# Differential attention on one core: the two softmaxes combined in chunks of 512 keys, spread over the steps of a round

## What is computed

```
sc = einsum('bqhd,bkhd->bhqk', qb, k) * scale         # 8 heads of 64, used in pairs
sc = where(k_chunk <= q_chunk, sc, lowest)            # causal by chunks of 64
pr = softmax(sc, axis=-1).reshape(b, 4, 2, 128, s)
a  = pr[:, :, 0] - lam * pr[:, :, 1]                  # two softmaxes, one difference
out = einsum('bhqk,bkhe->bqhe', a, v)                 # value width 128
```

## Time and profile before

| | |
|---|---|
| median of 3 runs | 1739.46 us (1738.71 to 1740.19) |
| the profiled execution | 1740.0 us, its span in the trace 1738.1 us |
| TensorE matmul busy | 1701.3 us, 98% of the span |
| TensorE weight loads busy | 1418.6 us, 82% |
| VectorE / ScalarE / GpSimd busy | 1087.6 / 665.6 / 272.3 us (63% / 38% / 16%) |
| granted TensorE clock | full speed (0.999) |
| attention, from its first score to its last gate product | about 779 to 1382 us |

### The profile page before, as it was taken

How to read it: one execution, slowest core, us unless ns; L and a number is a source line. 1 busy time by engine, 2 the same in 40 slices (tenths; PEclk the granted TensorE clock), 3 DMA queues, 4 the chain that set the end, 5 groups by cost and what they waited for, 6 DMA issues and landing times.

```text
span 1738.1 us, 22885 instructions
## 1 busy us (share of the span) xinstructions
PE 1701.3 (98%) x8296; PEld 1418.6 (82%) x8296; DVE 1087.6 (63%) x2151; ACT 665.6 (38%) x1184; POOL 272.3 (16%) x194
## 2 busy tenths in 40 slices
PE   7999999999999999999999998999999899999998
PEld 6888888888788888888888887888888788888887
DVE  5538566645877877747777776777867453424242
ACT  5423233224333323215455454554555442323231
POOL 0000000265522332311110022111111040000000
PEclk9999999999999999999999999999999999999999
DMA  7447999754425433297677558856567865353532
GB/s 242 139 162 298 384 350 335 251 155 144 146 76 167 120 99 114 80 293 242 197 202 233 137 165 247 248 172 179 167 176 224 290 232 189 109 182 112 180 111 71
DMA packets 161886, 331.04 MB, mean 190 GB/s; under 512 B 15714, under 2 KB 60770, under 8 KB 156258
## 3 DMA queue, kind: packets, MB, share of 16 engines
q1 hardware_dynamic: 160610, 327.38, 59.4%
q10 hardware_dynamic: 1152, 2.10, 0.3%
HBM read 218.26 MB, written 111.16 MB: 190 GB/s over the span
## 4 chain that ended last, share of the span: by engine, by line
PE 87%; DVE 5%; DMA 3%; issue 2%; POOL 1%; ACT 1%; SPq 1%; DVEq 0%; ACTq 0%
PE bank L1245 14%; PE bank L1246 14%; PE bank L1247 14%; PE bank L1422 13%; PE bank L1327 5%; PE bank L1329 5%; PE bank L1330 5%; PE bank L1382 5%; PE bank L1354 3%; PE bank L1355 3%; PE bank L1365 3%; DVE e L2181 2%; DVE at_lo L2217 1%; PE bank L1255 1%; PE bank L1402 1%
## 5 line engine op out<-in xcount | busy, mean ns | idle before, releaser
L1327 PE MATMUL bank<-ht,a_op 128*128 128x512 f32 x504 | 196.3, 390 | 2.4 <-DVE stage L1958 1.2
L1330 PE MATMUL bank<-ht,a_op 128*128 128x512 f32 x504 | 196.1, 389 | 0.0
L1329 PE MATMUL bank<-ht,a_op 128*128 128x512 f32 x504 | 196.1, 389 | 0.0
L1720 ACT ACTIVATE e<-e,nbias 128x128 f32<-128x128 f32 (+15 forms) x128 | 153.6, 1200 | 80.7 <-DVE nbias L2190 80.6
L2181 DVE CUSTOM_DVE_ANT_0 e<-bank,zeros 128x512 f32<-128x512 f32 x192 | 124.9, 688 | 90.3 <-PE bank L1355 90.1
L1245 PE MATMUL bank<-ht,w 128*128 128x512 f32 x448 | 174.4, 389 | 0.0
L1246 PE MATMUL bank<-ht,w 128*128 128x512 f32 x448 | 174.3, 389 | 0.0
L1247 PE MATMUL bank<-ht,w 128*128 128x512 f32 x448 | 174.3, 389 | 0.0
L1422 PE MATMUL bank<-ht,w 128*128 128x512 f32 x624 | 168.7, 395 | 0.0
L1229 POOL TENSOR_SCALAR mask<-kc,qc 128x128 f32<-128x128 f32 (+3 forms) x64 | 87.7, 1370 | 495.8 <-DVE mx L2181 495.3
L1382 PE MATMUL bank<-at_hi,v_sl 128*128 128x256 f32 (+1 forms) x576 | 118.9, 285 | 14.7 <-DVE at_lo L2217 14.2
(11 more groups left out here) (188 smaller groups left out, 3515.7 us busy)
## 6 DMA issues: line engine op xcount, KB each, us to landing
w<-split_s SPq DMA_DIRECT2D x92, 512.0 KB, 4.8
raw<-in_w_in SPq DMA_DIRECT2D x64, 512.0 KB, 5.4
split_s<-piece SPq DMA_DIRECT2D x24, 1024.0 KB, 5.7
q_st<-qk_s SPq DMA_DIRECT2D x128, 128.0 KB, 4.9
ring<-gate_s SPq DMA_DIRECT2D x64, 256.0 KB, 3.4
ht_s<-ht SPq DMA_DIRECT2D x6, 2048.0 KB, 9.5
gate_s<-gate_st SPq DMA_DIRECT2D x48, 256.0 KB, 4.9
qk_s<-stage SPq DMA_DIRECT2D x48, 192.0 KB, 3.9
```

The source lines that it names most:

```text
L1327: nc.tensor.matmul(out[:], hi, right[:, k, 0, :], start=k == 0 and not adds, stop=False, skip_group_check=adds)
L1329: nc.tensor.matmul(out[:], hi, right[:, k, 1, :], start=False, stop=False, skip_group_check=adds)
L1330: mm = nc.tensor.matmul(out[:], lo, right[:, k, 0, :], start=False, stop=k == 3, skip_group_check=adds)
L1720: nc.scalar.activation(e, e, ACT.Exp, bias=nbias[G % 2][:, h:h + 1], scale=SCALE, accum_out=esum[G % 2][:, h:h + 1]).then_inc(exp_done, 1)
```

## The change

The combine of tile R is cut into its chunks. Chunk 0 (with the reciprocal and the ratio) stays at step 1; chunk i goes to step i+1, behind that step's `at_split`, but to the last step where the round has no step i+1. A turn now waits for its own chunk's combine, and the counters are counted in chunks instead of tiles.

```diff
 def turn(G, c, wide):
-    if c == 0:
-        pe.wait_ge(combined, G + 1)
     o = plan.before(G) + c // BLK
+    pe.wait_ge(combined, o + 1)
...
 def mask_max(G, c, wide, h):
-        dve.wait_ge(combined, G - 1)
+        dve.wait_ge(combined, plan.before(G - 1))
...
-def combine(G):
-    s1, s2 = esum[G % 2][:, 0:1], esum[G % 2][:, 1:2]
-    dve.wait_ge(exp_done, 2 * (G + 1))
-    nc.vector.reciprocal(ratio[:, 0:1], s2).then_inc(recip_done, 1)
...
-    a, b = e1[G % 2][:, 0:plan.keys(G)], e2[G % 2][:, 0:plan.keys(G)]
+def combine(G, c, wide):
+    if c == 0:
+        s1, s2 = esum[G % 2][:, 0:1], esum[G % 2][:, 1:2]
+        dve.wait_ge(exp_done, 2 * (G + 1))
+        nc.vector.reciprocal(ratio[:, 0:1], s2).then_inc(recip_done, 1)
...
+    a, b = e1[G % 2][:, c:c + wide], e2[G % 2][:, c:c + wide]
     nc.vector.scalar_tensor_tensor(out=a, in0=b, scalar=ratio[:, 1:2], in1=a, op0=ALU.mult,
                                    op1=ALU.add).then_inc(combined, 1)
...
-                        if 0 <= R < TILES and j == min(1, len(steps) - 1):
-                            combine(R)
+                        for i, chunk in enumerate(plan.chunks(R) if 0 <= R < TILES else ()):
+                            if j == min(i + 1, len(steps) - 1):
+                                combine(R, *chunk)
```

More of the change, by code:

```diff
@@ L2190, in neg_max @@
                     nc.vector.tensor_scalar(nbias[G % 2][:], m2[:], -SCALE, None, ALU.mult).then_inc(nb_ready, 1)
-                def combine(G):
-                    s1, s2 = esum[G % 2][:, 0:1], esum[G % 2][:, 1:2]
-                    dve.wait_ge(exp_done, 2 * (G + 1))
-                    nc.vector.reciprocal(ratio[:, 0:1], s2).then_inc(recip_done, 1)
[L2196 to L2199, removed]
-                    a, b = e1[G % 2][:, 0:plan.keys(G)], e2[G % 2][:, 0:plan.keys(G)]
+                def combine(G, c, wide):
[3 more added lines that the diff above has]
+                        nc.vector.reciprocal(ratio[:, 0:1], s2).then_inc(recip_done, 1)
+                        dve.wait_ge(recip_done, G + 1)
+                        nc.vector.scalar_tensor_tensor(out=ratio[:, 1:2], in0=ratio[:, 0:1], scalar=lam[:, 0:1], in1=s1,
+                                                       op0=ALU.mult, op1=ALU.mult).then_inc(ratio_ready, 1)
+                        dve.wait_ge(ratio_ready, G + 1)
+                    a, b = e1[G % 2][:, c:c + wide], e2[G % 2][:, c:c + wide]
                     nc.vector.scalar_tensor_tensor(out=a, in0=b, scalar=ratio[:, 1:2], in1=a, op0=ALU.mult,
```

## The result

The changed kernel takes 1742.82 us in the median of 21 runs (1740.05 to 1747.4), the kernel before, on the same chip at the same time, 1740.19 us (21 runs, 1736.37 to 1745.25). The ratio is 1.0017, with a 95% interval of 1.0009 to 1.0024: **slightly slower, by 3 us on the mean**, where -0.3 us was forecast. The time lies in the forecast range; its sign is that of neither my own case nor its rival C. The profiled executions differ by much less than the runs do: 1740.56 us (span 1738.7) against 1740.0 (span 1738.1).

A forecast was written before the change was run, and what follows sets the result against it. TensorE was taken as the bound, with only 28 us of waits for `at_lo` to win. A gain of 10.5 us and a loss of 10.2 us gave -0.3 us, forecast 1739.2 us, range 1733 to 1745.

The forecast's parts named there:

- my own case: Whole kernel: gain and loss nearly cancel, -0.3 us, reaching from -5 to +4; chance 0.65, no sign claimed.
- rival C: Step 1 of even rounds: the bias's lateness is taken up, the 10.5 us gain remains, 1729 us; chance 0.17.
- What bounds the kernel: Attention: time can come only from TensorE's waits, 28.0 us in 38 waits of the values for `at_lo`.
- The price of a piece: Combine on VectorE: a cut costs 0.13 us (bounds 0 to 0.22); 96 more instructions, 12.5 us more VectorE.
- What goes away: Step 3 of even rounds: values' waits behind the whole combine go, 5.25 us per half, 10.5 us in all.
- What comes in: End of odd rounds: last pieces delay the bias and next even round's values, 5.3 and 4.9 us, 10.2 us loss.
- Even rounds' later bias: End of even rounds: bias 0.4 to 0.7 us later, covered in odd rounds; uncovered, up to 8 us.
- The sum: Whole kernel: -10.5 + 10.2 = -0.3 us, forecast 1739.2 us.
- kind two: Step 1 of even rounds: values of chunk 0 wait for a split chained from the round before; rest of the 28 us.
- A: Start of rounds 8 to 24: reserves not to be had, 9.0 us per half reach the values, +7.5, 1747 us; chance 0.15.
- B: End of odd rounds: GpSimd's mask blocks the pieces on VectorE, 14*1.6 = 22 us, 1761; chance 0.03.
- D: Attention: nothing happens, pieces still run one behind another, 1739 us; counted with my own case, 0.65.

The follow-up runs named there:

- bias first: Changed kernel, but in odd rounds the last step's pieces are combined after `neg_max`, `scaled_eps` and `norm_o`; 1741.5 us, 1.0009 to the kernel before.
- cut only: Combine cut into pieces as in the change, but all pieces together at step 1; 1748.14 us, ratio 1.0052 to the kernel before.
- the earlier load: Load of `z_in` issued one round earlier, at the top of the odd round: kernel before 1740.03 us (0.9997), changed kernel 1744.87 us (1.0024).

## Why the prediction was right or wrong, step by step

- **What bounds the kernel: right.** The attention's time is in the waits for `at_lo`, and the runs that move them move the time: 19.6 us of them at 1732.6 us, 27.5 at 1742.8, 32.8 at 1748.1, 37.3 at 1752.9. It is no law to a few us: the kernel before has 28.0 at 1740.2, bias first 23.9 at 1741.5. And "no other wait of the attention counts for much" was wrong, see the sum below.
- **The price of a piece: right.** 0.12 to 0.14 us for a cut in the run with the cuts alone (forecast 0.13); 14.0 us more busy time for 96 instructions (forecast 12.5). The Trainium skill (VectorE: DVE Perf Modes, section on the TRN2 errata) is right in direction, that many small tiles pay a latency each time. The 60 ns that I took from its table are half of what the trace shows for this instruction, and the section itself says that this row comes out too low.
- **What goes away: right, 9.8 us for 10.5.** Six of the eight waits a half are gone. In round 20 0.34 us stay (forecast 0.32), in round 24 0.22 of 0.22: I had counted that one as gone.
- **What comes in: right, 10.7 us for 10.2.** Rounds 14, 16 and 18 wait 1.51, 2.15 and 1.91 us (forecast 1.4, 2.0 and 1.7), counting the scores' part. The claim that a wait at the scores would mean I was wrong was too strict: it appeared (2.7 us in six waits), but it lies in front of the same values and is a part of the same lateness. What it does show is that VectorE itself is late, not only ScalarE, as the run with the bias first confirms.
- **Even rounds' later bias: harmless, as said.** It was to come 0.4 to 0.7 us later. In the kernel with even rounds alone it comes 1.1 to 1.4 us later behind the last mask_max of rounds 8 to 22, and the loss is 0.
- **The sum: the step that failed.** It was -10.5 + 10.2 = -0.3 us, and the runs show about +3 (2.6 by the medians). Two terms were a little off: -9.8 + 10.7 = +0.9 us. "With the rounding of a dozen terms I do not claim a sign" was fair for this part. But the sum ended with the rounds and put everything else at nothing. It had no term for the junction at round 32 and the end of the attention, where TensorE waits for transfers, and where length and granted clock (+1.0 to 1.7 us by the runs' means) changed with nearly every edit. The row with the 2.84 us wait was in the view of waits as the longest of the 38. I counted it with the waits of kind two, though a transfer stands behind it, and gave it no term because the change doesn't touch it. At the end of the attention the view had a second line of this sort, which I took for nothing. It is the wait of 2.54 us that the kernel before has in front of its stretch at half the clock:

```profile
PEld bank L1399 <- ACT o_sq L1737: 3.6, 3, 2.5
```

Why the changed kernel has more time at half the clock at these places is open.
- **The base.** 1739.46 us was a median of three; 21 runs gave 1740.19. A further 0.7 us of the distance from 1739.2 to 1742.8 is that.
- **The rivals.** A, the late bias unsoftened, would have had a loss of 9.0 per half; 5.6 were measured, so the reserves of the earlier trace rows are real. B did not happen: the mask beside the pieces of round 15 (GpSimd at 923.84 for 1.15 us, VectorE from 924.13) left the two of them at 1.41 us, which is 0.66 + 0.75, so nothing was lost. The exclusion that the Trainium skill states (SBUF — State Buffer, section on who interferes with whom) doesn't show in this pair of instructions. C is excluded by the loss of 10.7. D, that nothing happens, is excluded by the traces.

The better version is the change in even rounds only: 0.9953 and 0.9966 in two sets, 6 to 8 us faster than before. In odd rounds TensorE multiplies no values and so waits for no split behind the combine; spreading wins nothing there and puts up to 1.33 us in front of the chain to the next values.

## What to carry to other kernels

Cut a long instruction only where something that the bottleneck waits for stands behind it in the queue; in the rounds where nothing does, its pieces end up in front of the next chain. List both kinds of place from the trace before cutting, and apply the edit by kind (here by the round's parity): two edits of opposite sign can sum to nothing and look like a change without effect. And where a gain and a loss cancel to a microsecond, the places that the change doesn't touch but that wait for transfers can weigh as much as what is left: they need a line in the sum, with a range.

## What the runs showed of the hardware that I had not expected

- TensorE's granted clock fell to the lower level for 3.4 us, or twice that, in or behind the long waits at the junction and at the end of the attention. Each such stretch of 3.4 us cost about 1.7, an estimate from the two levels, and five weight loads behind it took 1.82 us in place of 1.11. The length of the wait doesn't decide it alone: at the junction the clock fell behind 3.60 and 2.62 us (the changed kernel, twice) and 5.17 us (with the earlier load), and stayed up behind 2.84 us (the kernel before), 3.30 us (cut only) and 3.71 us (the kernel before with the earlier load). What does is open.
- By runs of one kernel: the kernel before took 1739.2 us where its granted clock was 0.999 (12 runs of the second set) and 1741.6 us at 0.998 (8 runs), so part of the spread of a single kernel is this. The three runs at 0.997 took 1741.1, so it isn't all of it.
- Removing a wait for one transfer at a place where all 16 DMA engines are busy (share 1.08) moved the wait to the next transfer with its full length: 2.84 + 0.67 us became 0.48 + 3.71, and the time stayed (0.9997).
